# Forget-gate attention scores: from two plain passes per head pair to four rounded passes on stacked halves

## The reference, cut to what matters

```python
def _fox_attend(q, k, v, log_f):
    B, S, H, d = q.shape
    nb = S // BLOCK_Q
    c = jnp.cumsum(log_f, axis=1)
    ...
    def block(args):
        i, q_b, cq_b = args
        s = jnp.einsum('bqhd,bkhd->bhqk', q_b, k, preferred_element_type=jnp.float32) * (d ** -0.5)
        s = s + cq_b[..., :, None] - ck[:, :, None, :]
        qpos = i * BLOCK_Q + jnp.arange(BLOCK_Q)
        s = jnp.where(kpos[None, :] <= qpos[:, None], s, NEG_INF)
        w = jax.nn.softmax(s, axis=-1).astype(v.dtype)
        return jnp.einsum('bhqk,bkhd->bqhd', w, v)
    ...

def _odd_mixer(x, w_in, b_f, w_out):
    B, S, _ = x.shape
    q, k, v, f = _split(x @ w_in, ODD_SPLIT)
    log_f = jax.nn.log_sigmoid((f + b_f).astype(jnp.float32))
    o = _fox_attend(...)
    return o @ w_out
```

## Time and profile before

| | us |
|---|---|
| median of three runs | 2226.6 |
| lowest, highest | 2226.48, 2228.15 |
| the profiled execution, its own time | 2229.03 |
| its span | 2227.1 |
| TensorE busy | 2175.7 (98%) |
| VectorE busy | 1238.0 (56%) |
| ScalarE busy | 896.6 (40%) |
| GpSimd busy | 220.8 (10%) |

### The profile page before, as it was taken

How to read it: one execution, slowest core, us unless ns; L and a number is a source line. 1 busy time by engine, 2 the same in 40 slices (tenths; PEclk the granted TensorE clock), 3 DMA queues, 4 the chain that set the end, 5 groups by cost and what they waited for, 6 DMA issues and landing times.

```text
span 2227.1 us, 27722 instructions
## 1 busy us (share of the span) xinstructions
PE 2175.7 (98%) x10139; PEld 1720.1 (77%) x10141; DVE 1238.0 (56%) x1991; ACT 896.6 (40%) x1498; POOL 220.8 (10%) x145
## 2 busy tenths in 40 slices
PE   7999999999999999999999999999999999999998
PEld 5767788888777777788888778678778787888887
DVE  5676643244375554643244377388489678542554
ACT  3555443243254545443243265432543444321332
POOL 0000400001300000400000330143000231000000
PEclk9999999999999999999999999999999999999999
DMA  6113233333223331333333144123212142333231
GB/s 174 26 45 97 76 94 106 92 94 104 85 77 87 98 104 45 94 95 107 91 94 104 57 134 114 48 85 104 78 54 80 51 120 70 105 100 98 85 104 67
DMA packets 351395, 197.45 MB, mean 89 GB/s; under 512 B 20896, under 2 KB 340141, under 8 KB 351294
## 3 DMA queue, kind: packets, MB, share of 16 engines
q1 hardware_dynamic: 350882, 196.03, 30.7%
q10 hardware_dynamic: 412, 0.07, 0.0%
HBM read 193.93 MB, written 2.14 MB: 88 GB/s over the span
## 4 chain that ended last, share of the span: by engine, by line
PE 85%; DVE 8%; issue 3%; ACT 3%; ACTq 0%; POOL 0%; DVEq 0%; POOLq 0%
PE PB L411 20%; PE PB L413 20%; PE PB L412 20%; PE PB L494 2%; PE PB L1407 2%; PE PB L1408 2%; PE PB L1409 2%; PE PB L540 2%; PE PB L513 2%; PE PB L1623 2%; PE PB L1624 2%; PE PB L1622 2%; DVE ATT L2992 1%; PE PB L1294 1%; DVE WL L381 1%
## 5 line engine op out<-in xcount | busy, mean ns | idle before, releaser
L375 ACT ACTIVATE WH<-RAW 128x1024 fp32r<-128x1024 f32 (+3 forms) x355 | 358.3, 1013 | 367.6 <-PE PB L413 273.4
L411 PE MATMUL PB<-XH,WH 128*128 128x512 f32 x1232 | 487.2, 395 | 5.9 <-DVE X L2427 1.9
L413 PE MATMUL PB<-XH,WL 128*128 128x512 f32 x1232 | 480.2, 390 | 0.0
L412 PE MATMUL PB<-XL,WH 128*128 128x512 f32 x1232 | 479.6, 389 | 0.0
L391 DVE TENSOR_TENSOR WL<-RAW,WH 128x1024 fp32r<-128x1024 f32 x172 | 220.7, 1284 | 148.4 <-ACT WH L375 146.6
L411 PEld LDWEIGHTS PB<-XH,WH 128*128 128x128 f32 x1232 | 230.9, 187 | 60.2 <-issue 3.3
L413 PEld LDWEIGHTS PB<-XH,WL 128*128 128x128 f32 x1232 | 230.8, 187 | 49.4
L412 PEld LDWEIGHTS PB<-XL,WH 128*128 128x128 f32 x1232 | 231.1, 188 | 47.4 <-issue 0.7
L381 DVE TENSOR_TENSOR WL<-RAW,WH 128x1024 fp32r<-128x1024 f32 (+2 forms) x163 | 195.6, 1209 | 105.8 <-ACT WH L375 105.1
L411 PE MATMUL PB<-HH,WH 128*128 128x512 f32 x512 | 199.2, 389 | 0.0
L412 PE MATMUL PB<-HL,WH 128*128 128x512 f32 x512 | 199.2, 389 | 0.0
(11 more groups left out here) (514 smaller groups left out, 3534.3 us busy)
## 6 DMA issues: line engine op xcount, KB each, us to landing
RAW<-in_w_up SPq DMA_DIRECT2D x64, 512.0 KB, 4.0
RAW<-in_w_down SPq DMA_DIRECT2D x64, 512.0 KB, 3.9
RAW<-in_w_ffn_gate_up SPq DMA_DIRECT2D x44, 512.0 KB, 3.8
RAW<-in_w_gate SPq DMA_DIRECT2D x32, 512.0 KB, 4.0
RAW<-in_od_w_in SPq DMA_DIRECT2D x24, 512.0 KB, 6.5
RAW<-in_w_in SPq DMA_DIRECT2D x24, 512.0 KB, 4.0
RAW<-in_w_ffn_down SPq DMA_DIRECT2D x22, 512.0 KB, 3.3
RAW<-in_ple_w_gate SPq DMA_DIRECT2D x16, 512.0 KB, 3.9
```

Source lines behind the costliest of these rows:

```text
L375: act.activation(WH[:, s, 0:nb], RAW[:, s, 0:nb], ACT.Copy).then_inc(hi_done[s], 1)
L411: pe.matmul(PB[b][0:m, 0:n], WH[:, s, k, 0:m], rh[:, kk, :], start=kk == 0, stop=False)
L412: pe.matmul(PB[b][0:m, 0:n], WH[:, s, k, 0:m], rl[:, kk, :], start=False, stop=False)
L413: x = pe.matmul(PB[b][0:m, 0:n], WL[:, s, k, 0:m], rh[:, kk, :], start=False, stop=kk == last)
```

## The change

The scores are no longer made from plain 32-bit operands. Keys and queries are split into a rounded high and a low part, as the weights are. For each head one stationary operand `QTWO` of 128 rows holds the high part of the queries on the head's own 64 rows and the low part on the other 64. `KHIGH` and `KLOW` hold the keys' high part twice, and their low part twice, once in either half. Two rounded passes then give all four products: `QTWO` by `KHIGH` and `QTWO` by `KLOW`. (VectorE's operation makes the low part as -0.125 times the bank minus the high part.)

Who makes what: ScalarE writes the high parts from the bank (two instructions of 64 rows for the keys, two for the queries) and copies the keys' high parts to the other half (two more); VectorE writes the keys' low parts (two), copies them to the other half (two), and writes the queries' low parts (two). The bank of keys and that of queries are now freed by VectorE.

Along with it: the parts come in the order keys, queries, values; the pieces per step are 7, 6, 7 and 4 blocks instead of 6 each; on ScalarE, the rounding of the weight tile stands behind the copies out of the bank and not ahead of them; and at the start, the turn of the first values stands behind the scores of step 0, as does VectorE's copy of them. `QTWO` and `KHIGH` lie where `ACC` is, `KLOW` where `QF` and `KF` were.

Semaphore names are left out of the diff.

```diff
@@ -196,8 +196,9 @@
         top[0] = mixer
         OH = region("OH", [P, DT, T], F32R)
         OL = region("OL", [P, DT, T], F32R)
-        QF = region("QF", [P, 2, T], F32)
-        KF = region("KF", [P, 2, T], F32)
+        KLOW = region("KLOW", [P, 2, 2, T], F32R)
+        QTWO = at("QTWO", [P, 2, 2, T], F32R, acc_at)
+        KHIGH = at("KHIGH", [P, 2, 2, T], F32R, acc_at + 8192)
         BC = region("BC", [P, 2, 2, T], F32)
         VP = region("VP", [P, 2, TT, P], F32)
         FZ = region("FZ", [16, 5, T], F32)
@@ -447,7 +448,7 @@
                 return QS[r, h // 2], K2[r, h // 4], lambda j: VS[:, j, h // 4 * 64:h // 4 * 64 + 64]
             if kind == "fox":
                 pp = h // 2 % 2
-                return QF[r, pp], KF[r, pp], lambda j: VP[:, pp, j, h % 2 * 64:h % 2 * 64 + 64]
+                return QTWO[:, pp, h % 2], (KHIGH[:, pp, h % 2], KLOW[:, pp, h % 2]), lambda j: VP[:, pp, j, h % 2 * 64:h % 2 * 64 + 64]
             if kind == "dsa":
                 return SQ_[r, h // 2], SK2[r], lambda j: SV[:, j]
             return MQ[r, h // 2], MK[r, h // 2], lambda j: MV[:, j, h * 64:h * 64 + 64]
@@ -479,8 +480,9 @@
                 if ns[e] >= 2:
                     wait(pe, score_read(ns[e] - 2), ns[e] - 2)
             if kind == "fox" and qb == 0:
-                evac_of(pe, M_FOX + 3 * g)
                 evac_of(pe, M_FOX + 3 * g + 1)
+                pe.wait_ge(sem["k_hi"], cnt.value("k_hi", (g, "twice", 1)))
+                pe.wait_ge(sem["k_lo"], cnt.value("k_lo", (g, 1)))
             if kind == "swa" and qb == 0:
                 evac_of(pe, M_A["q", g])
             if kind == "mla" and qb == 0:
@@ -491,6 +493,10 @@
                 pe.wait_ge(sem["chain_a"], cnt.value("chain_a", "krope"))
             for e in range(2):
                 q, k, _ = operands(kind, 2 * g + e)
+                if kind == "fox":
+                    for part, keys_of in enumerate(k):
+                        pe.matmul(PB[2 + e][:, 0:w], q[:, qb * P:qb * P + P], keys_of[:, 0:w], start=part == 0, stop=False)
+                    continue
                 xs[e] = pe.matmul(PB[2 + e][:, lo:lo + w], q[:, qb * P:qb * P + P], k[:, ks[0] * P:ks[0] * P + w], start=True, stop=plain)
                 if plain:
                     done(xs[e], "scores", ns[e])
@@ -1108,7 +1114,7 @@
             W = wview("od_w_in")
             loadn(W[:, :, 3072:3088], 8, 16)
             for j in range(8):
-                for c in range(3):
+                for c in (1, 0, 2):
                     loadn(W[:, :, c * D + j * P:c * D + j * P + P], 8, P)
                 if j == 0:
                     continue
@@ -1857,7 +1863,6 @@
             assert st.m == M_FOX
             for _ in project():
                 pass
-            turn_values(0)
             ahead = [project() for _ in range(7)]
             unfinished = []
 
@@ -1878,12 +1883,12 @@
                 if j and qb == 0:
                     turn_values(j)
                 if j < 7:
-                    for _ in range(6):
+                    for _ in range((7, 6, 7, 4)[qb]):
                         next(ahead[j])
                 else:
                     for _ in range((4, 4, 3, 3)[qb]):
                         next(outs_ahead)
-            pe_attend(pe, ("fox",), 8, project_ahead)
+            pe_attend(pe, ("fox",), 8, project_ahead, start=lambda: turn_values(0))
             p_turn(1)
             for _ in outs_ahead:
                 pass
@@ -2384,17 +2389,25 @@
 
             def project(j, part):
                 pp = j % 2
-                step()
+                lin_ready(act, st)
                 b, ub = st.bank(0)
                 if part == 0:
-                    x = act.activation(QF[:, pp], PB[b][:], ACT.Copy, scale=-0.125)
+                    for e in range(2):
+                        r = slice(e * 64, e * 64 + 64)
+                        done(act.activation(KHIGH[r, pp, e], PB[b][r], ACT.Copy), "k_hi", (j, e))
+                    for e in range(2):
+                        r, other = slice(e * 64, e * 64 + 64), slice((1 - e) * 64, (1 - e) * 64 + 64)
+                        act.wait_ge(sem["k_hi"], cnt.value("k_hi", (j, e)))
+                        done(act.activation(KHIGH[other, pp, e], KHIGH[r, pp, e].bitcast(F32), ACT.Copy), "k_hi", (j, "twice", e))
                 elif part == 1:
-                    x = act.activation(KF[:, pp], PB[b][:], ACT.Copy)
+                    for e in range(2):
+                        r = slice(e * 64, e * 64 + 64)
+                        done(act.activation(QTWO[r, pp, e], PB[b][r], ACT.Copy, scale=-0.125), "q_hi", (j, e))
                 else:
                     if j:
                         act.wait_ge(sem["misc"], cnt.value("misc", ("vp", j - 1)))
-                    x = act.activation(VT[:], PB[b][:], ACT.Copy)
-                x.then_inc(evac[b], 1)
+                    act.activation(VT[:], PB[b][:], ACT.Copy).then_inc(evac[b], 1)
+                hi_ahead(act, st)
                 nxt()
             for part in range(3):
                 project(0, part)
@@ -3217,18 +3230,39 @@
             done(dve.memset(FZ[:, 0], 1.0), "chain_d", "fone")
             dve.wait_ge(sem["chain_d"], cnt.value("chain_d", "fone"))
             done(dve.tensor_tensor_scan(FZ[:, 3], FZ[:, 0], FZ[:, 2], 0.0, ALU.mult, ALU.add), "fox_c", 0)
+            def fox_lows(j, part):
+
+                b, ub = st.bank(0)
+                pp = j % 2
+                if part == 0:
+                    dve.wait_ge(sem["k_hi"], cnt.value("k_hi", (j, 1)))
+                    for e in range(2):
+                        r = slice(e * 64, e * 64 + 64)
+                        x = dve.tensor_tensor(KLOW[r, pp, e], PB[b][r], KHIGH[r, pp, e].bitcast(F32), ALU.subtract)
+                    x.then_inc(evac[b], 1)
+                    dve.wait_ge(evac[b], ub + 1)
+                    for e in range(2):
+                        r, other = slice(e * 64, e * 64 + 64), slice((1 - e) * 64, (1 - e) * 64 + 64)
+                        done(dve.tensor_copy(KLOW[other, pp, e], KLOW[r, pp, e]), "k_lo", (j, e))
+                elif part == 1:
+                    dve.wait_ge(sem["q_hi"], cnt.value("q_hi", (j, 1)))
+                    for e in range(2):
+                        r, into = slice(e * 64, e * 64 + 64), slice((1 - e) * 64, (1 - e) * 64 + 64)
+                        x = dve.scalar_tensor_tensor(QTWO[into, pp, e], PB[b][r], -0.125, QTWO[r, pp, e].bitcast(F32), ALU.mult, ALU.subtract)
+                    x.then_inc(evac[b], 1)
+                lo_ahead(dve, st)
+                nxt()
             for part in range(3):
-                skip()
-            token_major(("vp", 0), VP[:, 0])
+                fox_lows(0, part)
 
             def project_ahead(c):
                 j, qb = divmod(c, TT)
                 if qb:
                     if j < 7:
-                        skip()
+                        fox_lows(j + 1, qb - 1)
                 elif j:
                     token_major(("vp", j), VP[:, j % 2])
-            dve_attend(dve, ("fox",), 8, project_ahead)
+            dve_attend(dve, ("fox",), 8, project_ahead, start=lambda: token_major(("vp", 0), VP[:, 0]))
             p_low(1)
 
             def residual_fox(o):
```

More of the change, by code:

```diff
@@ L92 @@
  topk hsp hg_x hg_prod hg_read hg_e hg_d hg_o hg_small hx mn m2 varb ln_v x_full sum7q pj pj_free memsum cross xsum
- asum ysum h_up quad mvt yt yo ot_in xt_in z r_tok merge os brf var_out var_in dn dn_free gain_in tok_ss tok_y tok_rt""".split()
+ asum ysum h_up quad mvt yt yo ot_in xt_in z r_tok merge os brf q_hi k_hi k_lo var_out var_in dn dn_free gain_in tok_ss tok_y tok_rt""".split()
 def program(nc, known, t):
```

## The result

The changed kernel takes **2235.4 us** (median of 7 runs, 2234.2 to 2237.3), the kernel before 2226.9 (7 runs beside it, 2226.5 to 2229.5): a ratio of 1.0035, 95% interval 1.0026 to 1.0044. By the ratio it is slower by 7.8 us (5.8 to 9.8), by the two medians 8.5; 4.8 were forecast. The profiled execution took 2236.17 us with a span of 2234.4. Two later executions, one of run 2 and one of the kernel before beside runs 5 to 8, took 2425 and 2429 us at a mean clock of 0.849 and 0.948 and are left out of the ratios.

A forecast was written before the change was run, and what follows sets the result against it. TensorE was taken to bound the forget-gate stage: -5.8 us for score passes, +9.5 for seven waits, +1.1 at the start, in all +4.8, giving 2231.4 us; wide range 2225.5 to 2235.5, the forecast's own 2229 to 2233.5.

The forecast's parts named there:

- What bounds the stage: Forget-gate stage: TensorE busy in all 25.37 us per head pair, so passes removed or waits added count one for one.
- The score passes: Forget-gate scores: steps of 0.91, 0.70, 0.48 and 0.48 us at 512, 384, 256 and 128 keys; 5.8 us saved.
- the rival of 0.213: 128-key scores: rounded passes take 0.213 us like plain ones instead of 0.12; 2.6 us more, 2234.0 us; chance 0.22.
- The rival of weight loads in the open (2253.8): Score steps: a 0.187 us load stands before each of four passes in 30 steps, 22.4 us more; chance 0.02.
- The walk to the new wait: Keys' and queries' steps, instruction by instruction: late 512-key minimum delays the queries' bank; TensorE waits 1.35 us before 128-key scores.
- The holds at a change of the start row: ScalarE and VectorE copies alternating halves: each starts only after the one before ends, so priced end to start.
- The rival in which the copies overlap: Key and query copies: no hold when rows change, so the wait is 0.88 us; 2228.1 us; chance 0.20.
- the wait: TensorE before the next pair's 128-key scores, for the queries' bank: 1.35 us in each of 7 pairs, 9.5 us.
- bank free and seen at 13.20: Queries' step: VectorE's operations end at 13.16 us behind the 384-key scores; TensorE can start at 13.20.
- The start: Start of the stage: next projection pass about 1.1 us later because weight rounding and low part precede the first minimum.
- The queries in time: Before the 128-key scores: queries' bank freed under 11.85 us, so no wait, -4.7 us, 2221.9 us; chance 0.11.

The follow-up runs named there:

- run 2: Changed kernel with VectorE's low part of the weight tile moved behind the queries' operations from the second pair on: 2226.4 us, ratio 0.9991.
- runs 5 to 8: One chip: changed kernel again 2235.1; first values' turn restored, weights rounded early 2234.4; early rounding plus 7, 8, 7, 2 blocks 2223.3; old kernel, new projection order 2228.3 us.
- runs 3 and 4: Changed kernel with other projection blocks per step: 7, 8, 7, 2 (TensorE six passes later) 2226.9 us; 6, 6, 6, 6 (three passes earlier) 2241.6 us.
- run 1: Changed kernel with ScalarE's rounding of the weight tile put back ahead of the first pair's values' copy: 2232.7 us, ratio 1.0021.
- run 5: The changed kernel measured again, nothing altered, on another chip: 2235.1 us, ratio 1.0031.
- runs 3 and 7: Changed kernel with 7, 8, 7, 2 blocks per step: 2226.9 us; the same plus the first pair's weight tile rounded ahead of the values' copy: 2223.3 us.
- run 8: Kernel before, plain scores kept, with only the new order of projections and 7, 6, 7, 4 blocks per step: 2228.3 us, ratio 1.0001.
- run 4: Changed kernel with 6 blocks of projections in each step, TensorE three passes earlier at the 128-key scores: 2241.6 us, ratio 1.0065.

## Why the prediction came out as it did

- **What bounds the stage** was right: each wait put in front of TensorE came out in the time, as runs 3 and 4 show from both sides.
- **The score passes** cost what was said: 0.91, 0.70, 0.48 and 0.47 us; 5.8 saved. The pass of 128 columns, with no row before, runs every 0.11 to 0.14 us, so the value taken (0.12) held and the rival of 0.213 is false. The rival of weight loads in the open (2253.8) is false too: the 128-key passes, each with a load of its own on the same rows, leave no room for 0.187 us. What the Trainium skill says in "TensorE: Matmul & The Clock Gate", Part 3, on loads that overlap only across row groups, these rows contradict again (the same Part also names a background weight buffer that a load can go to, and that clause they do not contradict); its other rule there, that two half-height tiles run side by side, agrees with the rows of the kernel before; the changed scores have no half-height tiles and do not test it.
- **The walk to the new wait** held at each step, in times behind the 384-key scores (742.51): TensorE's 512-key scores at 5.36 (5.37 said), minimum at 8.03 (7.99), queries' operations from 11.86 to 13.25 (11.77 to 13.16), TensorE there at 11.84 (11.85). The holds at a change of the start row are in the rows, on VectorE (1.39 for two of 0.69) and on ScalarE (1.20 for two of 0.59). The rival in which the copies overlap is false.
- **The term that was mis-sized is the wait: 1.62 us, not 1.35, in seven pairs 11.3, not 9.5.** Of the 0.27 per pair, 0.09 is the chain's small lateness and the rest the step "bank free and seen at 13.20": I took 0.04 us from the end of VectorE's second operation to TensorE's first pass, and it is 0.21 (755.76 to 755.97). What fills the 0.21 us no run takes apart; it is 0.21 or 0.22 in runs 2, 3 and 4 too. This makes 1.8 of the 3.0 us between the forecast difference of 4.8 and the measured 7.8.
- **The start** cost 0.9 us (1.1 said), for the reason said; run 1 shows the cause.
- **Not in the sum**: the stretch at half clock, 1.3 us in the profiled execution. Since runs 2 and 8 have it and run 5 does not, it comes in some executions of any of these kernels, and a single profile can't charge it to the change.
- **The time came out near the edge.** The pair was to last about 25.9 us and lasts 26.21; 2235.4 is 4.0 above the forecast of 2231.4, outside the forecast's own range (2229 to 2233.5) and 0.1 inside the wide one. Its upper end, 2235.5, was made for narrow passes as slow as plain ones together with a longer wait; the narrow passes are not slow. That the wide range holds the result is in part luck; what was right is the chain. (Its lower end has a slip: a wait of 0.6 us per pair gives 2226.1 by the forecast's own sum, not 2225.5.)
- **The queries in time**, the rival of the other side, had the right condition and wrong odds only as to this kernel: where the condition is met (run 2, the low part out of the way; runs 3 and 7, more cover), the wait falls to 0.37 and 0.26 us and the time to that of before or below. The 2221.9 it named needs the wait wholly gone; with the start mended too, 2223.3 is what I got.

What is left over: the medians differ by 8.5 us in the first measurement and by 7.3 beside run 5, the stage by 6.2 without the half clock. The mean granted clock of each execution is on record beside its span, and sorts them. Beside run 5, executions at 0.998 have a mean span of 2226.6 us before the change (11 of them) and 2232.6 after it (5): 6.0 apart, as the stage is. But 11 of the 23 executions before the change ran at 0.999, with a mean span of 2225.1, and none of the 14 of the changed kernel (10 at 0.998, three at 0.997, one at 0.996). So the rest of the difference goes with the clock: the changed kernel had more time at the lowered clock per execution. Why, by its idle times or only because its waits fall at other moments, stays open.

## What to carry to other kernels

When work is moved onto idle engines, the question is not whether they are idle but what stands in their queues between the one result that the busy engine waits for and its source: here a 1.2 us operation that nobody needed for several us, ahead of a minimum, cost 1.25 us per pair, and moving it behind cost nothing. In the same place it had cost nothing before, when the queue ahead of it was shorter. Walk that chain instruction by instruction, compare its end with the time at which the busy engine arrives, and if it is late, either take the uninvolved work out of the chain or move work of the busy engine ahead of the wait; here each pass moved was worth its full 0.227 us, down to a wait of 0.26. Give the last step, from VectorE's end to the first pass that waited for it, a price from a row of its own: it is 0.21 us behind the queries, but 0.14 behind the minimum at the start of the stage (682.26 to 682.40), and 0.04 was too little here.

## What the runs showed of the hardware that was not expected

- **The half clock comes in some executions and at some places only.** At the start of the stage, three of the ten traces have it: the changed kernel's first (after an idle time of 2.16 us), run 2 (2.16) and run 8 (0.73 twice); seven don't, among them runs 3, 4 and 5 with the same 2.16. Windows of 20 us over the whole span show that the kernel before has such stretches as well, elsewhere (0.91 is the mean; in windows of 1 us the clock is 0.50 from about 130.5 to 133.5 and from 253 to 256.5):

```profile
120.00:140.00 20.00, 17.14 (x100) 13.06 (x100) 13.82 (x41) 13.13 (x38) 0.00 (x0) 0.91 0.25 60
240.00:260.00 20.00, 16.84 (x59) 12.18 (x60) 13.53 (x20) 9.57 (x14) 11.30 (x9) 0.91 0.06 17
```

  The changed kernel's first trace has three (from 120, 680 and 1740 us), run 5 two (240 and 1740). TensorE is idle for some time in or before each of them (17.14 and 16.84 us busy of 20 here); the waits of 1.6 us in the pairs were followed by none in the traces of the changed kernel, those of 2.1 in run 4 twice out of seven. The stretches whose cost the stage lengths give cost 1.2 (run 8) to 1.6 us (run 4), so one trace against another is uncertain by about that.
- **Rounded passes of 128 columns** start every 0.11 us, those of 256 every 0.12: below 256 columns a pass gets hardly shorter, while 384 and 512 take 0.174 and 0.227.
- **ScalarE holds at a change of the start row like VectorE**: two operations of 0.59 us take 1.20, and within SBUF two take 1.27. The first copy within SBUF writes to the same rows as the operation before it, and only its input starts at others; it starts 0.09 us before that one's end (746.83 against 745.72 + 1.20).
